# A padding tensor of 448 bytes per partition cut to 320 bytes, in a kernel that fuses two transformer blocks

## The chip, the cores and the metric

One core of a Trainium2 chip runs the whole kernel. The metric is the device time of one execution in microseconds (us), as the median of several runs. Engines: PE is the matmul engine (PEld its loading of weights), DVE the vector engine, ACT the scalar engine, POOL the engine for constants and small vectors, SP the queue that issues the weight transfers.

## The reference

Input x has 256 tokens of 1024 float32 features. It passes a first block, then a second block of two layers.

```python
def first_block(x, ...):
    h = rms_norm(x, norm_g[l])
    z = h @ w_in[l]                                  # ten parts, 9216 columns
    o_r = retention(q_r, k_r, v_r)                   # 8 heads, chunks of 128
    y_r = (rms_norm(o_r) * silu(gate_r)) @ ret_w_o
    o_d = diff_attention(rms_norm(q_d), rms_norm(k_d), v_d, lam)   # 8 heads
    y_d = (rms_norm(o_d) * (1 - lam_init) * silu(gate_d)) @ diff_w_o
    m = sigmoid(mg_r) * y_r + sigmoid(mg_d) * y_d
    return x + m @ w_out

def second_block(x, ...):
    for layer in range(2):
        h = h + 0.5 * swiglu_ffn(rms_norm_2(h), w_gate, w_up, w_down)   # 1024 -> 2816 -> 1024
        u = rms_norm_2(h)
        h = h + (conformer_conv(u) if layer == 0 else attention(u))     # 31 taps | stick-breaking, 16 heads
        h = h + 0.5 * swiglu_ffn(rms_norm_2(h), ...)
        if layer == 0:
            k_shared, v_shared = split(rms_norm_2(h) @ w_kv)
    return rms_norm_2(h)
```

## The kernel before

Every weight matrix is streamed from memory once, in slabs of 1 MB, through four slots of the tensor raw. For each slab ACT makes a rounded high half whi (line 1169) and DVE the remainder wlo = raw - whi (line 1521), both in the one-pass float format fp32r. The activations are split in the same way into high and low halves (aT, bT, hT). PE then adds three products for every weight tile: high by high, low by high, high by low. SP issues the loads in program order, each as soon as DVE has freed its slot, two slabs ahead of PE.

PE has two ways to take a slab. In the projections and the down projections (function part, lines 616 to 618) the activations are the loaded weights, 128 by 128, and 512 columns of whi or wlo stream past them. In the gate and up projections (function wide_slab, lines 673 and 675) it is the other way round: 128 columns of whi or wlo are loaded, and aT streams past, 512 columns with both halves for whi and 256 for wlo. ACT copies the second half of that product out (low_part, line 1328), DVE adds and multiplies (act_out, hid, lines 1816 to 1833), ACT applies silu and makes the high half hT_hi (1337), and DVE makes the low half hT_lo (1839). The down projection reads hT_hi and hT_lo.

The order of stages: the first block with its two kinds of attention, run between slabs; feed-forward, convolution (its transforms in plain float32, lines 985 and 988), feed-forward, shared keys and values; feed-forward, attention, feed-forward. Semaphores written out by hand order everything, and each engine's list of instructions is fixed.

Memory is laid out in the order of allocation, each tensor at the next multiple of 32 bytes per partition. First come the tensors that live throughout: raw, whi, wlo (32 KB a partition each), h, aT, the identity, the gains and some small statistics, and last of all a tensor named align that no instruction uses. Behind it four sets of tensors share one region, one set after the other in time: first (rowbuf, qkT_d, v_r, bT, attw and others), second (act_out, hid, rsb, hT_hi, hT_lo, kT, vS, low_part), conv (u, spec, yn, pre, table) and stick (qT, sp, wexp). The start addresses per partition, worked out from the sizes and the 16,512 bytes that stand ahead of raw:

| tensor | start before | modulo 256 |
|---|---|---|
| raw, whi, wlo | 16512, 49280, 82048 | 128 |
| h, aT, ident | 114816, 123008, 139392 | 128 |
| align | 140992 | 192 |
| rowbuf, act_out | 141440 | 128 |
| hT_hi, hT_lo | 152192, 174720 | 128 |
| bT_hi, bT_lo | 198784, 206976 | 128 |
| low_part | 217728 | 128 |

Of the kernel before, what the change touches and what calls it, by code (L numbers as in the profile page):

```python
# [31 lines left out]
P = 128  # L32
# [113 lines left out]
def build(nc, A, out):  # L146
    with ExitStack() as ctx:
        def sb(name, shape, dt=F32, to=ctx):
            return to.enter_context(nc.sbuf_tensor(name, shape, dt))
# [24 lines left out]
        msq = sb("msq", [P, TT])  # L174
        dqk_g = sb("dqk_g", [P, 2])
        dqk_s = sb("dqk_s", [P, 2])
        sb("align", [P, 112])

        first = ExitStack()
        rowbuf = sb("rowbuf", [P, TT, D], to=first)  # L180
# [1996 lines left out]
```

How the kernel before makes its waits and increments, by code:

```python
        @block.sync  # L372
# [5 lines left out]
            def load(k, top, bottom, halves=2):  # L378
                if k >= SLOTS:
                    sp_.wait_ge(lo_ready, k - SLOTS + 1)
                for q, src in enumerate((top, bottom)):
                    dst = raw[:, k % SLOTS, :].rearrange("p (k n) -> p k n", n=CW)
                    dst = dst[:, 2 * q:2 * q + 2, :] if halves == 2 else dst[:, :, q * FW:(q + 1) * FW]
                    sp_.dma_start(dst, src).then_inc(tops_landed[k] if k < 3 and q == 0 else landed[k % SLOTS], 16)
# [52 lines left out]
                     rows(pw1, 4 * half, 4, slice(D + c * FW, D + (c + 1) * FW)), halves=1)  # L439
            square(p2a.k, A["conv_w_pw2_2"][0], [(c * CW, half) for c, half in pair_order(2)])
            ffn_named("ffn2a", "ffn2", 0)
            square(pkv.k, A["w_kv_2"], [(c * CW, half) for c, half in KV_ORDER])
            ffn_named("ffn1b", "ffn1", 1)
            square(pq.k, A["attn_w_q_2"][0], [(c * CW, half) for c, half in pair_order(2)])
            square(po.k, A["attn_w_o_2"][0], [(c * CW, half) for c, half in pair_order(2)])
            ffn_named("ffn2b", "ffn2", 1)
            for t in range(TT):
                sp_.wait_ge(out_left, t + 1)
                sp_.wait_ge(out_ready, t + 1)
                sp_.dma_start(out[0, t * P:(t + 1) * P, :], h[:, t, :]).then_inc(out_landed, 16)
            sp_.wait_ge(out_landed, 16 * TT)
# [250 lines left out]
            def exit_fills(b, g, half):  # L703
                pe.wait_ge(acc_free, 2 * g + 2)
                for q in range(2):
```

## Time and profile before

| | us |
|---|---|
| median of 3 runs | 1267.0 |
| lowest and highest | 1266.4, 1267.07 |
| the profiled execution, its own time | 1267.07 |
| its span from the first to the last instruction | 1265.3 |
| PE busy in it | 1256.4 |
| mean granted clock of PE | 0.999 |

The span is what the trace covers; the 1.8 us beside it lie around the instructions. A matmul's duration in the profile is modelled and reaches into the next one, so a busy PE says that PE always has work, and the distance between starts says how fast it goes.

### The profile page before, as it was taken

What the parts mean: (1) busy time and instruction counts of PE and PEld (TensorE: products, weight loads), DVE (VectorE), ACT (ScalarE), POOL (GpSimd) and SP (SyncE); (2) the same over time, 40 slices, a digit from 0 to 9 for tenths busy, and PEclk for the clock granted to TensorE, in tenths of its full rate; (3) what the DMA queues carried; (4) which work ended last, traced back from release to release, by engine and by line L of the source; (5) the groups of instructions that cost most, each with busy time, mean ns of one, the idle gap of its engine ahead of it and who ended that gap; (6) DMA issues with size and microseconds to landing.
All of it is one profiled execution on the core that took longest, in us unless ns stands there. A gap on an engine that the chain in (4) does not pass through costs nothing.

```text
span 1265.3 us, 16693 instructions
## 1 busy us (share of the span) xinstructions
PE 1256.4 (99%) x6828; PEld 1075.8 (85%) x6828; DVE 827.0 (65%) x953; ACT 617.3 (49%) x761; POOL 84.9 (7%) x122
## 2 busy tenths in 40 slices
PE   9999999999999999999999999999999999999998
PEld 7888877888988888879888889898888988988886
DVE  6565677667677656676776655566765666776753
ACT  5354567543555534453555543355553454555542
POOL 2223010101000002001000000000000110100000
PEclk9999999999999999999999999999999999999999
DMA  9654544456665567544565655656555513666540
GB/s 319 209 157 155 197 134 147 165 187 199 200 192 185 173 216 231 172 133 153 182 199 183 209 175 166 199 167 199 184 183 199 168 66 107 211 199 200 200 166 34
DMA packets 165387, 225.27 MB, mean 178 GB/s; under 512 B 7520, under 2 KB 106436, under 8 KB 165312
## 3 DMA queue, kind: packets, MB, share of 16 engines
q1 hardware_dynamic: 163488, 220.23, 53.4%
q0 software_dynamic: 1808, 3.98, 1.0%
q8 instruction: 54, 0.88, 0.3%
q14 instruction: 21, 0.17, 0.0%
q10 hardware_dynamic: 16, 0.00, 0.0%
HBM read 223.14 MB, written 1.05 MB: 177 GB/s over the span
## 4 chain that ended last, share of the span: by engine, by line
PE 97%; DVE 2%; ACT 1%; DMA 0%; issue 0%; SPq 0%; ACTq 0%
PE acc L675 15%; PE acc L616 15%; PE acc L618 15%; PE acc L617 15%; PE att L675 8%; PE acc L673 8%; PE att L673 4%; PE acc L649 2%; PE acc L653 2%; PE acc L651 2%; PE tp L696 1%; PE att L616 1%; PE att L617 1%; PE att L618 1%; DVE wlo L1521 1%; ACT whi L1169 0%
## 5 line engine op out<-in xcount | busy, mean ns | idle before, releaser
L1521 DVE TENSOR_TENSOR wlo<-raw,whi 128x2048 fp32r<-128x2048 f32 x205 | 467.6, 2289 | 163.5 <-ACT whi L1169 163.4
L1169 ACT ACTIVATE whi<-raw 128x2048 fp32r<-128x2048 f32 x205 | 388.9, 1913 | 93.4 <-PE acc L618 82.3
L675 PE MATMUL acc<-aT,whi 128*128 128x512 f32 x832 | 290.9, 391 | 0.0
L673 PE MATMUL acc<-aT,wlo 128*128 128x256 f32 x832 | 233.7, 281 | 0.0
L675 PEld LDWEIGHTS acc<-aT,whi 128*128 128x128 f32 x832 | 155.6, 187 | 33.8
L616 PE MATMUL acc<-whi,aT 128*128 128x512 f32 x432 | 172.7, 400 | 0.5 <-DVE wlo L1599 0.5
L618 PE MATMUL acc<-wlo,aT 128*128 128x512 f32 x432 | 168.8, 391 | 0.0
L617 PE MATMUL acc<-whi,aT 128*128 128x512 f32 x432 | 168.5, 390 | 0.0
L675 PE MATMUL att<-aT,whi 128*128 128x512 f32 x448 | 157.8, 391 | 0.0
L673 PEld LDWEIGHTS acc<-aT,wlo 128*128 128x128 f32 x832 | 157.3, 189 | 0.0
L616 PE MATMUL acc<-whi,hT_hi 128*128 128x512 f32 x348 | 135.7, 390 | 0.0
L617 PE MATMUL acc<-whi,hT_lo 128*128 128x512 f32 x348 | 135.5, 389 | 0.0
L618 PE MATMUL acc<-wlo,hT_hi 128*128 128x512 f32 x348 | 135.4, 389 | 0.0
L673 PE MATMUL att<-aT,wlo 128*128 128x256 f32 x448 | 125.5, 280 | 0.0
L675 PEld LDWEIGHTS att<-aT,whi 128*128 128x128 f32 x448 | 83.8, 187 | 18.4
L616 PEld LDWEIGHTS acc<-whi,aT 128*128 128x128 f32 x432 | 81.4, 188 | 18.2 <-issue 1.4
L618 PEld LDWEIGHTS acc<-wlo,aT 128*128 128x128 f32 x432 | 81.2, 188 | 17.4
L617 PEld LDWEIGHTS acc<-whi,aT 128*128 128x128 f32 x432 | 81.4, 188 | 15.8
L1328 ACT ACTIVATE low_part<-acc 128x512 f32<-128x512 f32 x52 | 31.0, 596 | 124.4 <-PE acc L675 124.4
L1182 ACT ACTIVATE aT<-tp,gain 128x256 fp32r<-128x256 f32 x68 | 26.8, 475 | 126.3 <-PE tp L696 126.3
L673 PEld LDWEIGHTS att<-aT,wlo 128*128 128x128 f32 x448 | 84.7, 189 | 0.0
L618 PEld LDWEIGHTS acc<-wlo,hT_hi 128*128 128x128 f32 x348 | 65.3, 188 | 13.5
(327 smaller groups left out, 1627.0 us busy)
## 6 DMA issues: line engine op xcount, KB each, us to landing
raw<-in_ffn_w_gate_dram SPq DMA_DIRECT2D x88, 512.0 KB, 4.1
raw<-in_ffn_w_up_dram SPq DMA_DIRECT2D x88, 512.0 KB, 5.2
raw<-in_ffn_w_down_dram SPq DMA_DIRECT2D x88, 512.0 KB, 4.8
raw<-in_w_in_dram SPq DMA_DIRECT2D x70, 512.0 KB, 4.8
raw<-in_conv_w_pw_dram SPq DMA_DIRECT2D x24, 512.0 KB, 4.9
raw<-in_w_kv_dram SPq DMA_DIRECT2D x16, 512.0 KB, 5.0
raw<-in_ret_w_o_dram SPq DMA_DIRECT2D x8, 512.0 KB, 4.3
raw<-in_diff_w_o_dram SPq DMA_DIRECT2D x8, 512.0 KB, 4.3
```

Source lines behind the costliest of these rows:

```text
L616: mm_(banks[t][:, :], tokens(Th, kt, t), hi_, start=first_ and j == 0, stop=False)
L617: mm_(banks[t][:, :], tokens(Tl, kt, t), hi_, start=False, stop=False)
L618: last = mm_(banks[t][:, :], tokens(Th, kt, t), lo_, start=False, stop=last_ and j == len(kts) - 1)
L649: mm_(dst, whi[:, slot, cols], aT_hi[:, kt, :], start=half == 0 and j == 0 and n == 0, stop=False, skip_group_check=True)
L651: mm_(dst, whi[:, slot, cols], aT_lo[:, kt, :], start=False, stop=False, skip_group_check=True)
L653: last = mm_(dst, wlo[:, slot, cols], aT_hi[:, kt, :], start=False, stop=half == 1 and j == SLAB_K - 1, skip_group_check=True)
L673: mm_(bank[:, 0:T], wlo[:, slot, cols], aT_hi[:, kt, :], start=half == 0 and j == 0, stop=False, skip_group_check=True)
L675: last = mm_(bank[:, :], whi[:, slot, cols], aT[:, kt, :, :].rearrange("p a n -> p (a n)"), start=False, stop=half == 1 and j == SLAB_K - ...
L1169: A_(whi[:, slot, :], raw[:, slot, :], ACT.Copy).then_inc(hi_ready, 1)
L1182: last = A_(dst[:, kt, :], tp[b % 2][:, q * T:(q + 1) * T], ACT.Copy, scale=gain[:, GROW[g] + kt:GROW[g] + kt + 1])
L1328: A_(low_part[:, up, :, :], ffn_pair(name, c, up)[:, :, T:CW], ACT.Copy)\
L1521: V.tensor_tensor(wlo[:, slot, :], raw[:, slot, :], whi[:, slot, :].bitcast(F32), ALU.subtract)\
```

## The change

The size of the unused tensor align goes from 112 to 80 float32 per partition. All that is allocated behind it starts 128 bytes lower in each partition. No instruction changes but for the addresses of its operands.

```diff
         dqk_g = sb("dqk_g", [P, 2])
         dqk_s = sb("dqk_s", [P, 2])
-        sb("align", [P, 112])
+        sb("align", [P, 80])
 
         first = ExitStack()
```

## Rows read from the trace of the kernel before

**Rows 1.** Page: busy us (share of the span), and the chain by engine

```profile
span 1265.3 us, 16693 instructions
...
PE 1256.4 (99%) x6828; PEld 1075.8 (85%) x6828; DVE 827.0 (65%) x953; ACT 617.3 (49%) x761; POOL 84.9 (7%) x122
...
PE 97%; DVE 2%; ACT 1%; DMA 0%; issue 0%; SPq 0%; ACTq 0%
```

**Rows 2.** Waits of PE: releaser, us in total, times, longest us

```profile
PE att L776 <- POOL ident L466: 1.6, 1, 1.6
PE acc L616 <- DVE wlo L1599: 0.5, 2, 0.3
PE tp L785 <- DMA h<-in_x_dram: 0.4, 1, 0.4
PE tp L922 <- DVE attw L1767: 0.4, 1, 0.4
PE att L616 <- DVE aT L1959: 0.2, 1, 0.2
```

**Rows 3.** Groups by form: out<-in, count | busy us, mean ns | idle before

```profile
L675 PE MATMUL acc<-aT,whi 128*128 128x512 f32 x832 | 290.9, 391 | 0.0
...
L617 PE MATMUL acc<-whi,aT 128*128 128x512 f32 x432 | 168.5, 390 | 0.0
...
L617 PE MATMUL acc<-whi,hT_lo 128*128 128x512 f32 x348 | 135.5, 389 | 0.0
L618 PE MATMUL acc<-wlo,hT_hi 128*128 128x512 f32 x348 | 135.4, 389 | 0.0
...
L617 PEld LDWEIGHTS acc<-whi,hT_lo 128*128 128x128 f32 x348 | 65.3, 188 | 13.5
...
L617 PE MATMUL acc<-whi,bT_lo 128*128 128x512 f32 x64 | 24.9, 389 | 0.0
```

**Rows 4.** Timeline of PE in a down projection, first and last of 15 (start, modelled us)

```profile
439.68 0.39 PE L618 MATMUL acc<-wlo,hT_hi 128*128 128x512 f32 x1
...
442.85 0.39 PE L617 MATMUL acc<-whi,hT_lo 128*128 128x512 f32 x1
```

**Rows 5.** Timeline of PE, convolution, first and last start of 13 records

```profile
550.73 1.02 PE L985 MATMUL acc<-spec,table 128*128 128x512 f32 x2
...
555.89 0.59 PE L985 MATMUL acc<-spec,table 128*128 128x512 f32 x1
```

**Rows 6.** Timeline of PE at the head of a down projection

```profile
433.74 0.40 PE L616 MATMUL acc<-whi,hT_hi 128*128 128x512 f32 x1
433.98 0.40 PE L617 MATMUL acc<-whi,hT_lo 128*128 128x512 f32 x1
434.21 0.39 PE L618 MATMUL acc<-wlo,hT_hi 128*128 128x512 f32 x1
```

**Rows 7.** Windows of PE: us, busy (matmuls), granted clock, DMA share, GB/s

```profile
446.00:452.00 6.00, 6.00 (x28) 1.00 0.89 291
1240.00:1246.00 6.00, 6.00 (x28) 1.00 0.01 3
```

**Rows 8.** Instructions by tile: ns min/median/max, first and last start us

```profile
L1839 DVE TENSOR_TENSOR hT_lo<-hid,hT_hi x44: 678/681/693, 336.9 to 1206.7; 128x512 fp32r<-128x512 f32 x44
...
L1328 ACT ACTIVATE low_part<-acc x52: 575/597/597, 332.1 to 1196.9; 128x512 f32<-128x512 f32 x52
...
L1816 DVE TENSOR_TENSOR act_out<-acc,low_part x28: 681/692/692, 335.0 to 1197.6; 128x512 f32<-128x512 f32 x28
```

**Rows 9.** Windows by stage: PE, PEld, DVE, ACT, POOL busy, clock, DMA

```profile
1010.00:1090.00 80.00, 79.99 (x545) 68.90 (x544) 58.49 (x71) 42.14 (x51) 9.79 (x20) 1.00 0.35 112
1090.00:1266.00 176.00, 169.63 (x920) 147.12 (x918) 105.50 (x97) 80.97 (x85) 0.00 (x0) 0.99 0.49 162
```

**Rows 10.** Page, DMA queues: packets, MB, share of 16 engines

```profile
q1 hardware_dynamic: 163488, 220.23, 53.4%
q0 software_dynamic: 1808, 3.98, 1.0%
```

## The prediction

> **What bounds the kernel now.** I read the busy table of the page first, then the chain that ended last, then who waited for whom on TensorE (PE), and only then single rows of the timeline. The busy table and the chain [rows 1] say the same thing: PE is busy 1256.4 of 1265.3 us, and 97% of the chain is PE. VectorE (DVE) and ScalarE (ACT) stand in it with 2% and 1%, that is about 25 and 13 us, 38 us together. The waits of PE [rows 2] are five, of 3.1 us in all, and none of them is on a weight transfer. So a change moves the time in one of two ways: it changes how long PE takes from one matmul to the next, or it lengthens something that PE already waits for.
>
> A matmul's duration in the profile is modelled and overlaps its neighbours, so the measure of PE is the pitch, the distance between starts. In a down projection of the feed-forward block [rows 4] 14 pitches take 442.85 - 439.68 = 3.17 us, 226.4 ns each, for 512 columns. The granted clock in that stage is 1.00 [rows 7], which is the 2.4 GHz level, and 512 columns at it are 213.3 ns, so 13 ns of each pitch are something else. The pitch does not depend on what the DMA engines do: two windows of 6 us hold 28 matmuls each, one at 291 GB/s and one at 3 [rows 7].
>
> **The change, part by part.** The padding tensor shrinks from 112 to 80 float32, 448 to 320 bytes per partition. No instruction is added, removed or reordered, no semaphore, no size of a transfer. Both sizes are multiples of the 32 bytes by which tensors are placed, so everything allocated after the padding starts exactly 128 bytes lower, and everything ahead of it (the weight slots raw, whi and wlo, the residual h, the operand aT, the identity) stays. Ahead of the change all large tensors, on both sides of the padding, begin at 128 modulo 256 bytes. After it the moved ones begin at 0 modulo 256 and the others still at 128. Slices are taken in steps of 256 bytes or multiples, so whole operands change with their tensors. What the change does is therefore only this: the moved operands start on another multiple of 128 bytes, and an instruction that mixes moved and unmoved tensors gets operands of two phases. All its possible costs are rates, which I take group by group.
>
> 1. *PE, unmoved operands only.* The 1280 pairs of the wide slabs (aT with whi and wlo) and the projections from aT [rows 3] read and write nothing that moved. Cost 0.
>
> 2. *PE, one moved operand.* The down projections take hT_hi or hT_lo as the loaded weights and whi or wlo as the moving operand: 3 x 348 = 1044 matmuls. Three groups of 64 take bT_hi or bT_lo, 192 more. Together 1236 matmuls [rows 3], at 226.4 ns some 280 us of the span. This is the only large exposed term. The trace has no large PE operand at 0 modulo 256, so it shows no price for it, and I bound it from both sides. From below: the plain float32 matmuls of the convolution run in two records per matmul, 12 of whose starts span 555.89 - 550.73 = 5.16 us, 430 ns a record [rows 5]. That is 2 x 213.3 and 3 ns for two passes of 512 columns, or 215 ns a pass, with both operands at 128 modulo 256. If the new phase took the 13 ns down to this, 1236 x 11.4 ns = 14.1 us would go. From above: slower pitches of the same form stand at the head of a down projection, where two take 434.21 - 433.74 = 0.47 us, 235 ns each [rows 6]. If every one of the 1236 had such a pitch, 1236 x 8.6 ns = 10.6 us would come. Between these I take 0, for three reasons out of rows. First, [rows 5] show that operands at 128 modulo 256 do not themselves cost the 13 ns, since those passes have such operands and do without them; the extra is a property of the form (one pass of fp32r per loaded weight), which stays. Second, loading the moved weights takes 188 ns [rows 3], which fits under the 226 ns of the matmul beside it, so a few ns on a load would be hidden. The cover is 38 ns; beyond it the pitch would follow the load one for one. Third, hT_lo, bT_lo and aT as loaded weights in line 617 give the same 389 to 390 ns modelled [rows 3], though they lie in quite different places and face different slots, so no conflict between a weight's address and a moving operand's address is to be seen at any of those distances.
>
> The Trainium skill, page "SBUF — State Buffer", section "Specifications (TRN2)", describes the memory as lines of 16 bytes where only crossing into a new line costs something. 128 bytes are eight such lines, and each operand keeps its place within a line, so by that rule the pitch is 226.4 ns as before and the sum is 0; by the rows alone it is 0 with the two ends above. No row of before tests the rule at another start address. It speaks against both PE rivals below.
>
> 3. *DVE and ACT on moved tensors.* Here the moved tensors are the gate, the hidden rows and their splits (about 0.6 to 0.7 us an instruction, [rows 8]), the softmax tiles and the first block's row buffers. Same forms stay within 678 to 693 ns, and 575 to 597 ns on ACT, beside every load on the other engines. Cost taken 0. What hides a change: DVE is busy for 60 to 73% of each stage (the two ends in [rows 9]), and PE has the next slab ready. What is exposed if it is not 0 is at most the share of the chain, 38 us; a tenth more on all of it is 3.8 us, a tenth less gives 3.8 us back. The longer end needs every DVE and ACT piece of the chain to be on a moved tensor, which is not so (the weight split L1521, 1% of the chain, is unmoved), so I keep 2 to 4 us for it. If more than the cover goes, the low halves of the weights come late and PE waits at the next slab.
>
> 4. *POOL and DMA.* Transfers into moved tensors are on POOL's queue, 3.98 MB and 1.0% of the engines' time [rows 10] (one more, 4 KB of a gain, is on ACT's), all for constants that are fetched ahead. The 220 MB of weights land in raw, which stays. PE's only wait on a transfer is 0.4 us, on x into h [rows 2], also unmoved. Cost 0; if all of them took a tenth longer, their 1.0% would become 1.1%, under work that is already there, and PE has no wait on any of them.
>
> The sum against the profiled execution: 1267.07 us for a span of 1265.3, so 1.8 us lie around it, plus 0 + 0 + 0 + 0. The three runs shown have a median of 1267.0 and lie within 0.7 us. Forecast 1267.0 us. A measurement of this kernel can tell about 0.2%, 2.5 us, from no change.
>
> **The rivals.** *A, the moved weights feed PE faster (ends on the other side).* Place: the 1236 matmuls of part 2. It would need the 13 ns above the columns' time to come from the start address of the loaded weights in this form only. For it: those 13 ns have no other explanation in a row. Against it: [rows 5]. Price up to 14.1 us, 1253 us; it decides from 2.5 us / 1236 = 2.0 ns a matmul. *B, mixed phases cost PE.* Same place, operands 128 bytes out of step where they were in step. For it: now every pair is in step, so the trace could not show such a conflict, and there is little to gain but all of it to lose. Pitches of 235 ns beside 226 exist [rows 6], so something can hold a matmul up by 9 ns. Against it: these come while every operand is in step, so they are not the mixed phase, and windows deep in a down projection are flat whatever else runs [rows 7]. Price up to 10.6 us, 1278 us; it decides from 2.0 ns too. A few ns would land at 1270 to 1273. *C, DVE and ACT get slower on moved tensors* (DVE's second input and its output out of step). Price 2 to 4 us, 1269 to 1271 us; it decides when the exposed 38 us grow by 6.6%. For it: two-input instructions of DVE run at one element a cycle and more (684 ns for 512) with everything in step. Against it: their spread is under 3% beside any load.
>
> The same page, section "Who interferes with whom", says that PE and ACT never wait for another user of the memory, which again is against B. The flat windows agree with it as far as they go; no run here shows the mixed phase.
>
> **How the numbers follow.** No change within 0.2%: 0.68, since the first term touches nothing that moved, the third and fourth are hidden but for a small part, and the second is 0 by the reasons given. B 0.14, C 0.07, A 0.11. B is put above A because in-step operands are all that the trace has seen, at a steady pitch. That gives faster 0.11, same 0.68, slower 0.21. The forecast's own range is 1264.5 to 1269.5 us, which holds 0.68; the small end of B and all of C, below 1274, bring some 0.13 more, and half a microsecond below takes in the smallest A. So 1264.0 to 1274.0.
>
> **What would show it.** Right: the pitch of [rows 4] again 226 to 227 ns, the groups of [rows 3] and [rows 8] within 1 or 2 ns of their means, the same five PE waits, every stage of [rows 9] as long as now. B or A: the groups with hT and bT change, those with aT do not, and the span changes by 1236 times the difference, in the down projections only. C: longer means at hT_lo, low_part and attw, with stages longer where PE waits for them, mainly in the first block. The prediction is wrong, too, if a group that touches no moved tensor changes; then the cause is not an operand's start address but something that moves with it.

## The result and the profile after

The changed kernel takes 1273.98 us (median of 6 runs, 1273.77 to 1275.18) against 1266.89 us for the kernel before in the same comparison (6 runs, 1266.40 to 1267.11). That is 7.1 us more, a ratio of 1.0058 with a 95% interval of 1.0048 to 1.0068. The profiled span grew from 1265.3 to 1271.8 us, 6.5 us, at the same mean granted clock of 0.999.

The page of the changed kernel, its span and its busy table:

```profile
span 1271.8 us, 16693 instructions
...
PE 1263.0 (99%) x6828; PEld 1075.1 (85%) x6828; DVE 827.1 (65%) x953; ACT 617.6 (49%) x761; POOL 85.0 (7%) x122
```

Beside [rows 1], PE is busy 6.6 us longer with the same 6828 matmuls, and the other engines are busy as long as before. The waits of PE after the change say that nothing new holds it up:

```profile
PE att L776 <- POOL ident L466: 1.6, 1, 1.6
PE acc L616 <- DVE wlo L1599: 0.7, 3, 0.3
PE tp L922 <- DVE attw L1767: 0.4, 1, 0.4
PE att L616 <- DVE aT L1959: 0.2, 1, 0.2
```

Four of the five waits of [rows 2] are there within 0.2 us; the fifth, 0.4 us on the transfer of x into h, is gone. The 6.6 us are in the groups by form (busy us, mean ns):

```profile
L675 PE MATMUL acc<-aT,whi 128*128 128x512 f32 x832 | 291.0, 391 | 0.0
...
L617 PE MATMUL acc<-whi,aT 128*128 128x512 f32 x432 | 168.3, 390 | 0.0
...
L616 PE MATMUL acc<-whi,hT_hi 128*128 128x512 f32 x348 | 137.7, 396 | 0.0
L617 PE MATMUL acc<-whi,hT_lo 128*128 128x512 f32 x348 | 137.4, 395 | 0.0
L618 PE MATMUL acc<-wlo,hT_hi 128*128 128x512 f32 x348 | 137.4, 395 | 0.0
...
L617 PEld LDWEIGHTS acc<-whi,hT_lo 128*128 128x128 f32 x348 | 65.3, 188 | 15.7
...
L617 PE MATMUL acc<-whi,bT_lo 128*128 128x512 f32 x64 | 25.2, 394 | 0.0
```

Against [rows 3] the three groups that load hT are busy 2.0, 1.9 and 2.0 us longer, 5.9 us together, and those that load bT 0.2 to 0.3 us each. The groups with aT, line 675 among them, have not moved by more than 0.4 us, and downwards where they did. The loads take 188 ns as before; what grew is the idle time between them, from 13.5 to 15.7 us in the group shown. The starts in a down projection (timeline of PE, same place as [rows 4]) show how:

```profile
443.80 0.39 PE L618 MATMUL acc<-wlo,hT_hi 128*128 128x512 f32 x1
444.03 0.40 PE L616 MATMUL acc<-whi,hT_hi 128*128 128x512 f32 x1
444.26 0.39 PE L617 MATMUL acc<-whi,hT_lo 128*128 128x512 f32 x1
444.49 0.40 PE L618 MATMUL acc<-wlo,hT_hi 128*128 128x512 f32 x1
444.73 0.39 PE L616 MATMUL acc<-whi,hT_hi 128*128 128x512 f32 x1
...
450.80 0.39 PE L618 MATMUL acc<-wlo,hT_hi 128*128 128x512 f32 x1
```

From the first row to the last are 30 pitches in 7.00 us, 233.3 ns each, where [rows 4] has 226.4. The modelled durations alternate, 0.39 and 0.40, which suggests that every second matmul is the slower one; the starts, printed to 10 ns, are too coarse to say so.

The modelled durations understate the loss. By the starts of PE over both whole timelines, the stretches with hT take 243.80 us in place of 237.10, 6.70 more, and those with bT 44.95 in place of 44.00, 0.95 more. All else behind the first bT stretch is as long as before (0.01 us in sum). The first 240 us are 1.2 us shorter, most of it in the first 9 us, where the kernel before waited 0.4 us for x. This part is 0 to 1.2 us shorter than before in all the runs below but e7, whatever was moved, and is taken as scatter. So the moved operands cost 7.65 us, and the spans differ by 6.5.

DVE and ACT on moved tensors kept their times (instructions by tile: ns min/median/max, beside [rows 8]):

```profile
L1839 DVE TENSOR_TENSOR hT_lo<-hid,hT_hi x44: 679/682/693, 336.7 to 1211.6; 128x512 fp32r<-128x512 f32 x44
```

```profile
L1328 ACT ACTIVATE low_part<-acc x52: 578/599/600, 331.8 to 1201.7; 128x512 f32<-128x512 f32 x52
```

### The profile page after: what moved, and what is told of

It is laid out like the page before. It is cut to its first block, busy times and chain, and to the rows that moved or that the text cites. A ratio compares the mean times of both kernels' runs of the same rounds, so it can differ in the third digit from the quotient of the medians.

```text
span 1271.8 us, 16693 instructions
## 1 busy us (share of the span) xinstructions
PE 1263.0 (99%) x6828; PEld 1075.1 (85%) x6828; DVE 827.1 (65%) x953; ACT 617.6 (49%) x761; POOL 85.0 (7%) x122
## 4 chain that ended last, share of the span: by engine, by line
PE 97%; DVE 2%; ACT 1%; issue 0%; POOL 0%; ACTq 0%; POOLq 0%; DVEq 0%
PE acc L675 15%; PE acc L616 15%; PE acc L618 15%; PE acc L617 15%; PE att L675 8%; PE acc L673 8%; PE att L673 4%; PE acc L649 2%; PE acc L653 2%; PE acc L651 2%; PE tp L696 1%; PE att L616 1%; PE att L617 1%; PE att L618 1%; DVE wlo L1521 1%; ACT whi L1169 0%
## 5 line engine op out<-in xcount | busy, mean ns | idle before, releaser
L675 PE MATMUL acc<-aT,whi 128*128 128x512 f32 x832 | 291.0, 391 | 0.0
L675 PE MATMUL att<-aT,whi 128*128 128x512 f32 x448 | 157.8, 391 | 0.0
```

What stands on the lines that cost most here:

```text
L675: last = mm_(bank[:, :], whi[:, slot, cols], aT[:, kt, :, :].rearrange("p a n -> p (a n)"), start=False, stop=half == 1 and j == SLAB_K - ...
```

## The experiments

Two theories were to be told apart first. *Relative*: a matmul is slowed when its loaded weights and the moving operand start at different places modulo 256 bytes. *Absolute*: what counts is where the loaded weights start. e1 and e2 tell them apart, and also a third, *timing*: it is not the operands of PE but something else that moved with the addresses. Below, the offset is the start of hT (and bT, where it moved too) minus the start of the weight slots, modulo 256; it is 0 before the change and 128 after it. Pitches are 30 starts of PE in the first down projection, about 443.8 to 450.8 us of each timeline. Every experiment was compared with the kernel before on the same chip; that one gave 1266.7 to 1266.9 us each time. The pitch of before is that of [rows 4], over 14 pitches; it is 226.7 ns in the runs that are in step. Averaged over all four down projections of a trace (1034 pitches) it is within 0.2 ns of the table in every run, and 226.8 before.

The second column names the operands that matter here. Other tensors move with them: h and the identity with the slots and aT (e1, e2), the identity with aT (e7), and kT, vS and low_part, which lie behind hT (e5, e6, f3).

| run | what starts where | offset | pitch, ns | us | ratio (95% interval) |
|---|---|---|---|---|---|
| before | all in step | 0 | 226.4 | 1266.89 | |
| after | hT, bT moved | 128 | 233.3 | 1273.98 | 1.0058 (1.0048 to 1.0068) |
| e1 | slots, aT, hT and bT moved | 0 | 226.7 | 1266.84 | 1.0001 (0.9992 to 1.0011) |
| e2 | slots and aT moved alone | 128 | 233.3 | 1274.33 | 1.0061 (1.0046 to 1.0076) |
| e3 | padding 96 | 192 | 229.0 | 1269.01 | 1.0017 (1.0008 to 1.0027) |
| e4 | padding 16 | 128 | 233.3 | 1273.79 | 1.0056 (1.0039 to 1.0073) |
| e5 | hT moved, bT not | 128 | 233.3 | 1273.07 | 1.0051 (1.0036 to 1.0066) |
| e6 | hT_lo alone | 0 and 128 | 231.0 | 1271.15 | 1.0034 (1.0021 to 1.0047) |
| e7 | aT alone | 0 | 226.7 | 1278.67 | 1.0095 (1.0080 to 1.0110) |
| e8 | padding 64 | 64 | 233.3 | 1274.49 | 1.0063 (1.0046 to 1.0080) |
| e9 | padding 104 | 224 | 233.3 | 1274.89 | 1.0063 (1.0050 to 1.0075) |
| e10 | padding 88 | 160 | 233.3 | 1282.60 | 1.0126 (1.0112 to 1.0140) |
| e11 | padding 72 | 96 | 234.3 | 1275.57 | 1.0070 (1.0055 to 1.0086) |
| e12 | padding 56 | 32 | 233.3 | 1274.36 | 1.0060 (1.0046 to 1.0074) |
| f1 | as e10, ones in step | 160 | 233.3 | 1274.68 | 1.0062 (1.0047 to 1.0077) |
| f2 | ones, rdiag, rsb alone | 0 | 226.7 | 1275.70 | 1.0070 (1.0055 to 1.0085) |
| f3 | hT_hi alone | 128 and 0 | 233.3 | 1273.39 | 1.0054 (1.0037 to 1.0071) |

**e1 and e2: is it the offset or the place?**

```diff
+        sb("front", [P, 32])
         raw = sb("raw", [P, SLOTS, SLAB_K * CW])
...
-        sb("align", [P, 112])
+        sb("align", [P, 48])     # e1; 80 in e2
```

> All weight slots and aT 128 bytes higher, hT and bT where the change put them, so every large operand starts at 0 modulo 256. Relative theory (a matmul is slowed when its loaded weights and its moving operand are 128 bytes out of step): pitch with hT 226 to 227 ns again, 1267 us. Absolute theory (weights loaded from a start at 0 modulo 256 cost 6.6 ns): pitch with hT 233 ns as after, and now the 1440 matmuls of 512 columns with aT loaded too (+9.5 us) and the 2560 of the wide slabs (up to +17 us), so 1283 to 1300 us. Timing theory (it is no matter of addresses in PE but of what moved around it): 1274 us, pitch with hT 233 ns.

> Weight slots and aT 128 bytes higher, hT and bT exactly at the addresses of before, so they are out of step the other way round. Relative theory: pitch with hT 233 ns, aT groups 227 ns, 1274 us. Absolute theory: pitch with hT 226 to 227 ns, aT groups 233 ns, 1276 to 1293 us.

e1 has hT exactly where the change put it and only the slots and aT moved after it; e2 has hT exactly where it was before. PE in e1, first and last of 31 starts (the added line shifts the line numbers by one):

```profile
443.78 0.39 PE L617 MATMUL acc<-whi,hT_hi 128*128 128x512 f32 x1
...
450.58 0.39 PE L617 MATMUL acc<-whi,hT_hi 128*128 128x512 f32 x1
```

and in e2:

```profile
443.81 0.39 PE L617 MATMUL acc<-whi,hT_hi 128*128 128x512 f32 x1
...
450.81 0.39 PE L617 MATMUL acc<-whi,hT_hi 128*128 128x512 f32 x1
```

6.80 us against 7.00 us for 30 pitches. The same weights at the same addresses are fast or slow according to where the slots start, and e1 gives back the whole loss. The absolute theory falls, and so does the timing theory: it forecast 1274 us for e1.

One rival is left by these two runs. The slots are also what ACT and DVE write and what the transfers fill, so an offset between hT and the slots could act through those engines. The trace of the changed kernel settles it: near the end of the last down projection PE works alone (window in us, its length, busy of PE, PEld, DVE, ACT and POOL, granted clock, DMA share, GB/s), and the starts are as far apart as elsewhere.

```profile
1250.00:1258.00 8.00, 8.00 (x36) 6.40 (x36) 0.00 (x0) 0.00 (x0) 0.00 (x0) 1.00 0.00 0
```

```profile
1250.05 0.39 PE L617 MATMUL acc<-whi,hT_lo 128*128 128x512 f32 x1
...
1255.65 0.39 PE L617 MATMUL acc<-whi,hT_lo 128*128 128x512 f32 x1
```

That is 24 pitches in 5.60 us, 233.3 ns each, with no other engine and no transfer active. The whole loss is there with PE alone.

**e3 and e4: another distance, and the period.** Only the size of align changes, to 96 and to 16.

> Padding 96 in place of 112: hT and bT 64 bytes lower, at 64 modulo 128, slots as before. Relative theory: some price, 1268 to 1274 us, according to how the price goes with the distance. Absolute theory: only a start at 0 modulo 256 costs, so 1267 us.

> Padding 16: hT and bT 384 bytes lower than before, at 0 modulo 256 but 256 modulo 512; slots as before. Relative and absolute theory with a period of 256 bytes: 1274 us, pitch with hT 233 ns. A period of 512 bytes: another value, 1267 us if only 0 modulo 512 costs. Timing theory: any value.

At an offset of 192 the pitch is 229.0 ns and the loss 2.2 us; at 384 bytes down, which is 128 modulo 256 again, it is that of the change. 128 and 384 bytes give the same, so no period of 512 bytes is seen. f2, further down, shows it from the other side: there hT starts 256 bytes higher than before and runs at 226.7 ns.

**e5: is it the down projections alone?**

```diff
+        sb("gap", [P, 32], to=second)
         hT_hi = sb("hT_hi", [P, FT, T], F32R, to=second)
```

> Padding 112 as before; a gap of 128 bytes just ahead of hT_hi puts hT_hi and hT_lo (and kT, vS, g_out, low_part behind them) 128 bytes out of step with the weight slots, while bT, act_out, hid, attw and all else of the first block stay. If the loss is PE's reading in the down projections: 1044 x 6.6 ns = 6.9 us, 1273.7 us, pitch with hT 233 ns, with bT 227 ns. Rival (part of the loss came with DVE, ACT or the first block's tensors): less than 6 us.

Groups by form in e5: hT slow, bT as before.

```profile
L618 PE MATMUL acc<-whi,hT_lo 128*128 128x512 f32 x348 | 137.4, 395 | 0.0
...
L618 PE MATMUL acc<-whi,bT_lo 128*128 128x512 f32 x64 | 24.9, 389 | 0.0
```

The loss is 6.35 us of 7.1, but its interval (4.6 to 8.4 us) is too wide to say where the rest is. The starts say it: the stretches with hT are 6.70 us longer than before, as in the changed kernel, those with bT 0.00 us in place of 0.95, and all else behind the first of them is within 0.1 us of before. Nothing is left for DVE, ACT or the transfers.

**e6 and f3: which of the two halves.** e6 puts the gap of e5 between hT_hi and hT_lo, f3 has one gap ahead of each.

> The gap of 128 bytes now behind hT_hi, so only hT_lo (and kT, vS, g_out, low_part) is out of step. Prefetch theory (the weights of the next matmul are read while the moving operand of this one streams): only the pitch of line 616, under which hT_lo is loaded, grows by 6.6 to 10 ns, 2.3 to 3.5 us in all, 1269 to 1270.5 us. Own-operand theory (the cost falls on the matmul that uses the weights): the pitch of line 617 grows instead, same sum. If the alternation of 230 and 237 ns is a matter of every load being out of step, the sum may be below a third of 6.9 us.

> hT_hi 128 bytes out of step with the slots, hT_lo in step (256 bytes higher). hT_hi is loaded for lines 616 and 618, hT_lo for 617. If a tile that is out of step slows the matmul before it and the one that uses it, all three pitches are touched: 4.5 to 7 us, 1271 to 1274 us. If loads add up one by one: two thirds of 6.9 us and the rest of what hT_lo alone cost, 4.6 us, 1271.4 us, with only two pitches grown.

In e6 the starts are these, three lines of code in turn (617 loads hT_hi, 618 hT_lo, 619 hT_hi):

```profile
443.62 0.39 PE L619 MATMUL acc<-wlo,hT_hi 128*128 128x512 f32 x1
443.85 0.40 PE L617 MATMUL acc<-whi,hT_hi 128*128 128x512 f32 x1
444.08 0.40 PE L618 MATMUL acc<-whi,hT_lo 128*128 128x512 f32 x1
444.31 0.39 PE L619 MATMUL acc<-wlo,hT_hi 128*128 128x512 f32 x1
```

A tile out of step lengthens the matmul ahead of it, under which it is loaded, and the one that uses it (0.40, 0.40, 0.39 in turn). The pitches averaged over the whole trace agree: 233.3 ns for lines 617 and 618, 226.8 for 619. So neither of my two readings held alone, and 4.4 us is more than the 2.3 to 3.5 I gave. With hT_hi alone out of step all three are touched (averages of 232.6, 230.8 and 236.4 ns), 233.3 ns as with both: the loss doesn't add up load by load, and it reaches its full size at two loads of three.

**e7: are other operands subject to it?**

```diff
         h = sb("h", [P, TT, D])
+        sb("front", [P, 32])
         aT = sb("aT", [P, KT, 2, T], F32R)
...
-        sb("align", [P, 112])
+        sb("align", [P, 80])
```

> aT and the identity 128 bytes higher, hT, bT and the slots where they were before. aT is loaded in lines 616 to 618 (1440 matmuls of 512 columns) and is the moving operand of 1280 pairs in the wide slabs and 768 of 256 columns. Relative theory: pitch of 616 to 618 with aT 233 ns (+9.5 us), of the wide pairs 6.6 ns or more longer for 512 columns (+8.4 us), hT 227 ns: 1277 to 1295 us. Rival (only tensors of hT's kind, written by DVE and ACT half a stage earlier, are sensitive): below 1269 us.

Groups by form: aT as loaded weights, 390 to 395 ns; aT as moving operand of the wide slabs, 391 to 393 ns; hT unchanged.

```profile
L676 PE MATMUL acc<-aT,whi 128*128 128x512 f32 x832 | 294.4, 393 | 0.0
...
L618 PE MATMUL acc<-whi,aT 128*128 128x512 f32 x432 | 170.8, 395 | 0.0
...
L618 PE MATMUL acc<-whi,hT_lo 128*128 128x512 f32 x348 | 135.5, 389 | 0.0
```

The cost follows the pair of operands, not the tensor. In the wide slabs 30 pairs take 10.53 us (351 ns each) where before they take 352.05 - 341.65 = 10.40 (346.7), so a pair loses 4.3 ns where a single matmul of a down projection loses 6.6. I had taken 6.6 ns there as well; the whole loss of 12.0 us lies at the low end of the 1277 to 1295 us expected.

**e8 to e12: every offset in steps of 32 bytes.** Only the size of align changes: 64, 104, 88, 72, 56.

> Padding 64: hT and bT 192 bytes lower, which is 64 bytes higher modulo 256. If only the distance without its sign counts, with period 256: as padding 96, 1269 us. If the price grows with the distance downwards: over 1274 us. If a period of 64 or 128 ruled, 1267 us, but padding 96 and 80 speak against it.

> Padding 104: hT and bT 32 bytes lower than in step, 224 bytes above the slots modulo 256. In step costs 0, 192 cost 2.1 ns a matmul, 128 and 64 cost 6.4 to 6.6. Curve theory (price falls steadily from 128 up to 256): 0.5 to 1.5 ns, 1267.3 to 1268.7 us. Exact-step theory (any offset at all costs at least 2 ns): 1269 us or more. A gain (in step is not the best place): below 1266.4 us.

> Padding 88: hT and bT 96 bytes lower, 160 above the slots modulo 256, between 2.1 ns (192) and 6.6 ns (128). Curve theory: 3 to 5 ns, 1270.5 to 1273 us. Exact-step theory with two levels: 1269 or 1274 us.

> Padding 72: 160 bytes lower, 96 above the slots modulo 256, between two neighbours of 6.5 ns. Both theories: 6 to 7 ns, 1274 us.

> Padding 56: 224 bytes lower, 32 above the slots modulo 256, between 0 (in step) and 6.5 ns (64). Curve theory: 3 to 4 ns, 1271 us. Exact-step theory: 6.5 ns, 1274 us, as at 64.

The steady curve that I expected is not there. Seven offsets have now been seen beside 0: 32, 64, 128, 160 and 224 give 233.3 ns, 96 gives 234.3, and 192 alone gives 229.0. 32 bytes out of step cost as much as 128. No offset beats being in step. And e10 went far outside its expectation, 1282.6 us.

**e10, f1 and f2: the same operands at two speeds.** In e10 the down projections lose what they lose elsewhere. The other 8 us are in the wide slabs, whose operands are all unmoved; groups by form, against 290.9 and 157.8 us before:

```profile
L675 PE MATMUL acc<-aT,whi 128*128 128x512 f32 x832 | 296.2, 398 | 0.0
...
L675 PE MATMUL att<-aT,whi 128*128 128x512 f32 x448 | 160.7, 398 | 0.0
```

The timeline of one stage of e10 shows where it begins. First a wide slab ahead of the two short plain matmuls on the tensor ones (line 737, four records in one row), then the wide slab behind them:

```profile
831.14 0.28 PE L673 MATMUL acc<-aT,wlo 128*128 128x256 f32 x1
831.25 0.39 PE L675 MATMUL acc<-aT,whi 128*128 128x512 f32 x1
831.48 0.28 PE L673 MATMUL acc<-aT,wlo 128*128 128x256 f32 x1
...
840.35 0.60 PE L737 MATMUL tp<-ones 128*128 128x128 f32 x4
...
841.14 0.28 PE L673 MATMUL acc<-aT,wlo 128*128 128x256 f32 x1
841.26 0.40 PE L675 MATMUL acc<-aT,whi 128*128 128x512 f32 x1
841.50 0.28 PE L673 MATMUL acc<-aT,wlo 128*128 128x256 f32 x1
```

0.34 us a pair ahead of them and 0.36 behind them, and it stays slow to the end of the gate and up projections. The other three feed-forward stages switch in the same way at line 687, which loads ones and streams rdiag: the pairs ahead take about 347 ns, the some 300 behind 353. In e10 ones and rdiag, which those plain matmuls load and stream, are 96 bytes below their place, so 160 above the slots and aT modulo 256; with each other they stay in step. f1 puts them back and keeps the rest of e10; f2 moves them alone:

```diff
-        sb("align", [P, 112])
+        sb("align", [P, 88])                # f1; 112 in f2
...
+        sb("gap24", [P, 24], to=second)     # f1; [P, 40] in f2
         ones = sb("ones", [P, P], to=second)
         rdiag = sb("rdiag", [P, TT, P], to=second)
         rsb = sb("rsb", [P, T], to=second)
+        sb("gap40", [P, 40], to=second)     # f1; [P, 24] in f2
         hT_hi = sb("hT_hi", [P, FT, T], F32R, to=second)
```

The areas of the convolution and of the attention begin 64 elements later in both, so that they stay clear of rsb.

> As padding 88, but ones, rdiag and rsb back at the addresses of before, and hT on the same offset modulo 256 as in padding 88 (one gap of 96 and one of 160 bytes; the areas of the convolution and of the attention begin 256 bytes later behind it). Entry theory (the plain matmuls on ones and rdiag, just ahead of the wide slabs, set the cadence into which they lock): wide pairs 346.7 ns again, 7.9 us less than with padding 88, near 1275 us. Write theory (DVE's and ACT's writes at the moved addresses of act_out, hid, hT slow PE): wide pairs 353 ns, 1282 us.

> Padding 112 as before, only ones, rdiag and rsb 160 bytes higher, hT and the rest behind it by a whole 256 bytes, so in step. Entry theory: wide pairs 353 ns in most feed-forward stages, hT pitch 227 ns, 1274 to 1275 us. Write theory, or an entry that needs more than the moved ones: wide pairs 346.7 ns, 1267 us.

Wide slabs, first and last of 30 pairs, in f1 (10.40 us, 346.7 ns a pair):

```profile
341.67 0.39 PE L677 MATMUL acc<-aT,whi 128*128 128x512 f32 x1
...
352.07 0.39 PE L677 MATMUL att<-aT,whi 128*128 128x512 f32 x1
```

and in f2 (10.60 us, 353.3 ns):

```profile
341.73 0.28 PE L675 MATMUL acc<-aT,wlo 128*128 128x256 f32 x1
...
352.33 0.28 PE L675 MATMUL att<-aT,wlo 128*128 128x256 f32 x1
```

f1 gives back 7.9 us of e10; f2, in which no heavy operand is out of step and hT runs at 226.7 ns, loses 8.95 us; by the starts of its trace it is 2.0 us in each of the four stages. So two short plain matmuls a stage set the speed of some 300 of its 320 pairs. The writes of DVE and ACT to act_out, hid and hT are not the cause: these are at moved addresses in f1 as well. rsb moved together with ones and rdiag and was not tried apart. Only DVE reads and writes it, and the slow pitch goes on in e10 between 842.10 and 843.81 us, where DVE is idle.

The other paddings bear on this too, since each of them moves ones and rdiag by the offset in the table. At 32, 64, 96, 128, 192 and 224 the wide slabs kept their speed (line 675 into acc is busy 290.9 to 291.0 us); of the seven offsets only 160 slows them.

## Why the prediction was wrong

*What bounds the kernel* was right: PE sets the time, and a change acts through the pitch or through a wait. All of the loss came through the pitch. *Parts 1, 3 and 4* held for this change: the groups with unmoved operands, DVE and ACT kept their times within 2 ns an instruction and 0.4 us a group, and e5 leaves nothing for them. For part 1 that is partly luck: with padding 88 (e10) groups whose operands are all unmoved lose 8.2 us by the starts.

*Part 2* is the step that failed, at "Between these I take 0". The place, the count of 1236 matmuls and the upper price were right: 10.6 us at most, measured 7.65 us by the starts (6.70 with hT, 0.95 with bT) and 7.1 us by the device time, while the modelled busy time shows 6.7 of it. The term put at 0 is 6.2 ns a matmul. Of the three reasons for 0, the third was empty. hT_lo, bT_lo and aT giving the same durations says nothing about a conflict of addresses when all of them start at 128 modulo 256, as do the slots; I had said so earlier in the same part and again under rival B, and then used it all the same. The second, a load of 188 ns under a matmul of 226, is true (187 to 188 ns in all runs, but for 192 in one group of e6) and does not protect: the pitch grew although the loads of the changed kernel did not. The first is left standing in so far as 226.7 ns is the lowest pitch of all seventeen kernels, with the operands at either start (before and e1).

*Rival B* is what happened, at two thirds of its price; it had 0.14 and no change had 0.68. The median of 1273.98 us lies just below the upper end of the range, 1274.0, which had been set for the small end of this rival and for rival C: that the range still holds it is luck, not the working of the sum. The reason that I gave for the rival, that a trace with everything in step cannot show the mixed case, should have weighed more than the flat windows of [rows 7]. These say only that the pitch does not depend on what the transfers do, and that holds out of step too: 233.3 ns with the transfers at work near 450 us and with none at 1250 us. *Rival A* falls with e1, in which the starts at 0 modulo 256 bring nothing. *Rival C* falls with the unchanged durations.

The Trainium skill, page "SBUF — State Buffer", section "Specifications (TRN2)", has lines of 16 bytes, from which I had concluded that 128 bytes would be free. The measurement decides against that conclusion: 32, 64 and 128 bytes, all whole lines, cost 6.6 ns a matmul (233.3 against 226.7 ns). The same page, section "Who interferes with whom", has PE waiting for nobody, and the page "TensorE: Matmul & The Clock Gate", section "Step-by-step: what each phase is for", has the load of the next weights take nothing from the running matmul since the two reads have ports of their own. The first may hold, for the interference is within PE: it depends on the starts of PE's two operands and is there while no other engine runs. The second does not hold here for fp32r: moving the loaded operand alone changes the pitch (e5), and one tile out of step slows the matmul under which it is loaded (e6).

Whether an address pattern or a clash in the memory stands behind the offset is open. What is shown is that the pitch in a long run takes one of a few steady averages (226.7, 229.0, 231.0, 233.3, 234.3 ns; 346.7, 351.0, 353.3 ns for a wide pair), that the offset of the operands decides it in the down projections, and that in the wide slabs what ran just before can decide it too. Why 192 costs less than its neighbours, and why 160 alone, of the offsets of ones and rdiag seen, puts the wide slabs into the slow pattern, is open. A version faster than the kernel before was not found; e1 equals it.

## What to carry to other kernels

When PE is the bound and works through long runs of load and matmul, keep the start of the loaded operand and of the moving one equal modulo 256 bytes (seen here for fp32r, 128 by 128 loaded under 512 columns), and after any change of the layout compare the pitch of long runs: the waits and the loads showed nothing of this, and the modelled busy time only a part. A trace in which all operands share one alignment is no evidence about any other, so the unseen case deserves its full range. If a group that touches nothing moved gets slower, look at what PE ran just before it.

## What the runs showed that was not expected

A pure shift of addresses moved this kernel between 1266.8 and 1282.6 us, 1.2%, with the same instructions. The pitch does not grow with the distance: 32 bytes cost as much as 128 (233.3 ns), 192 only 2.3 ns (229.0). Identical fp32r matmuls on identical addresses ran at 346.7 or 353.3 ns a pair for a whole stage, according to the addresses of two plain matmuls ahead of it (f1 and f2).
